# Moving ScalarE's rounding of gated tiles behind the next copy of turned probabilities

## What is computed

```python
for l in range(DEPTH):
    proj = einsum('bld,de->ble', h, w_in[l])
    a, g, zc, q, k, v, za, qi, ki, wi = split(proj)
    u = depthwise_conv(a * sigmoid(g)) + b_dw
    y_conv = silu(layer_norm(u, ln_g, ln_b)) * silu(zc)
    # attention over the 132 keys with the best index score, 8 heads of 64
    y_attn = sparse_attention(q, k, v, top 132 keys) * silu(za)
    y = concatenate([y_conv, y_attn]) @ w_out[l]
    h = layer_norm(alpha * h + y, post_ln_g[l], post_ln_b[l])
```

## Time and profile before

| what | value |
|---|---|
| median of 3 runs | 1014.51 us (1014.0 to 1015.2) |
| profiled execution | 1014.03 us, its span 1012.2 us |
| busy: TensorE | 982.5 us, 97% of the span |
| busy: VectorE | 668.4 us, 66% |
| busy: ScalarE | 559.6 us, 55% |
| busy: GpSimd | 232.4 us, 23% |
| mean granted clock of TensorE | 0.991 |
| attention loop of layer 0 | about 205 to 326 us |
| attention loop of layer 1 | about 514 to 640 us |

### The profile page before, as it was taken

The page is one execution under the profiler, slowest core; times in us unless marked ns, Lnnn a source line. Parts: engine busy times, 40 slices in busy tenths (PEclk is TensorE's granted clock), DMA queues, the critical chain, the costliest instruction groups (busy, mean ns, idle before and its releaser), DMA issues.

```text
span 1012.2 us, 15815 instructions
## 1 busy us (share of the span) xinstructions
PE 982.5 (97%) x6084; PEld 819.3 (81%) x6084; DVE 668.4 (66%) x1444; ACT 559.6 (55%) x920; POOL 232.4 (23%) x254
## 2 busy tenths in 40 slices
PE   8999999999999999999999999999999999999997
PEld 7888998986677988888878677888888788888886
DVE  4899999988673499999988756638522333333432
ACT  6685891655343568598165424544646566564442
POOL 0110671125212401077111511624101000000001
PEclk9999999999999999999999899999999999999999
DMA  8876885752001577487475300478777536366662
GB/s 299 198 183 169 214 195 135 174 118 85 1 1 66 143 186 175 121 192 183 125 170 122 118 21 1 169 172 199 180 215 198 116 87 162 88 162 129 173 160 83
DMA packets 23962, 143.92 MB, mean 142 GB/s; under 512 B 2880, under 2 KB 3648, under 8 KB 8272
## 3 DMA queue, kind: packets, MB, share of 16 engines
q0 software_dynamic: 8496, 60.36, 32.2%
q1 hardware_dynamic: 15392, 82.55, 23.0%
HBM read 140.81 MB, written 2.10 MB: 141 GB/s over the span
## 4 chain that ended last, share of the span: by engine, by line
PE 80%; DVE 10%; ACT 3%; issue 2%; POOL 2%; DMA 2%; SPq 1%; POOLq 0%; DVEq 0%; ACTq 0%
PE psum_B L1404 20%; PE psum_A L1404 13%; PE psum_B L1438 8%; PE psum_A L1438 8%; PE psum_A L1600 6%; DVE conv_acc L1918 4%; PE psum_C L1480 2%; PE psum_C L1404 2%; PE psum_A L1815 2%; PE psum_B L1815 2%; DMA w_raw<-in_weights 2%; PE psum_B L1544 2%; POOL w_lo L1184 2%; PE psum_B L1802 2%; PE psum_A L1516 2%
## 5 line engine op out<-in xcount | busy, mean ns | idle before, releaser
L1191 POOL DMA_DIRECT2D w_lo<-in_weights x59 | 52.0, 881 | 545.9 <-ACT w_lo L728 493.7
L1918 DVE SCALAR_TENSOR_TENSOR conv_acc<-u,vec,conv_acc 128x528 f32<-128x528 f32 (+1 forms) x240 | 172.4, 756 | 3.2
L1404 PE MATMUL psum_B<-x_hi,w_hi 128*128 128x272 f32 (+3 forms) x456 | 138.1, 337 | 0.5 <-ACT shifted L785 0.3
L1404 PE MATMUL psum_B<-x_hi,w_lo 128*128 128x272 f32 (+3 forms) x456 | 135.4, 331 | 0.0
L1404 PE MATMUL psum_B<-x_lo,w_hi 128*128 128x272 f32 (+3 forms) x456 | 135.3, 331 | 0.0
L727 ACT ACTIVATE w_hi<-w_raw 128x2048 fp32r<-128x2048 f32 (+2 forms) x73 | 113.4, 1553 | 25.8 <-DMA w_raw<-in_weights 25.3
L728 ACT ACTIVATE w_lo<-w_raw 128x2048 fp32r<-128x2048 f32 (+2 forms) x73 | 112.7, 1545 | 0.0
L1404 PE MATMUL psum_A<-x_hi,w_hi 128*128 128x272 f32 (+3 forms) x368 | 100.1, 315 | 0.8 <-DMA w_lo<-in_weights 0.4
L1404 PE MATMUL psum_A<-x_lo,w_hi 128*128 128x272 f32 (+3 forms) x368 | 98.1, 309 | 0.0
L1404 PE MATMUL psum_A<-x_hi,w_lo 128*128 128x272 f32 (+3 forms) x368 | 97.9, 309 | 0.0
L1404 PEld LDWEIGHTS psum_B<-x_hi,w_hi 128*128 128x128 f32 (+1 forms) x456 | 79.0, 187 | 10.0 <-issue 1.7
(11 more groups left out here) (409 smaller groups left out, 2294.9 us busy)
## 6 DMA issues: line engine op xcount, KB each, us to landing
w_raw<-in_weights SPq DMA_DIRECT2D x65, 1024.0 KB, 5.0
w_lo<-in_weights POOLq DMA_DIRECT2D x57, 1024.0 KB, 8.3
x_first<-in_x_t SPq DMA_DIRECT2D x8, 264.0 KB, 6.3
h<-in_x SPq DMA_DIRECT2D x1, 2048.0 KB, 9.8
out<-h SPq DMA_DIRECT2D x4, 512.0 KB, 2.6
w_raw<-in_weights SPq DMA_DIRECT2D x2, 512.0 KB, 7.6
post_ln_g<-in_post_ln_g SPq DMA_DIRECT2D x2, 512.0 KB, 4.6
post_ln_b<-in_post_ln_b SPq DMA_DIRECT2D x2, 512.0 KB, 6.3
```

What stands on the lines that cost most here:

```text
L1191: pool.dma_start(wlo[n % RING][:, 0:width], io["weights"][n, :, 0:width], accum_op=ALU.add) \
L1404: mm = pe.matmul(ps[0:cols, i, o:o + b - a], w[wp][:, kt, at:at + cols], x[xp][:, kt, a:b], start=(kt == 0 and wp + xp == 0), stop=(kt == ...
L1918: got = dve.scalar_tensor_tensor(dst, src, w, dst, ALU.mult, ALU.add)
```

## The change

ScalarE's loop used to round gated tiles in `woven`, at the end of a turn and so ahead of the next turn's first copy. Now `woven` leaves the roundings out, and a new function `gated` rounds what the two items of the turn before have, right behind the next turn's first copy and ahead of its two exponentials. The other steps of `woven` (the tanh, the meta rows' pairing, the squares) stay. 16 of the 18 roundings move (9 in layer 0, 7 in layer 1); the last of each layer, behind the loop, stays. The orders of TensorE, VectorE, GpSimd and SP are unchanged.

```diff
--- before.py
+++ after.py
@@ -995,7 +995,10 @@
                             pair_meta((l, part), meta_pair[1], slice(0, CT) if part == "conv" else slice(CT, KD), META)
                         elif op[0] == "tanh":
                             conv_tanh(l, op[1])
-                        elif op[0] == "hi":
+
+                def gated(i):
+                    for op in todo[i]:
+                        if op[0] == "hi":
                             y_hi(l, *op[1:])
 
                 def gates(i):
@@ -1005,6 +1008,9 @@
 
                 for i in range(0, n, 2):
                     take_probs_t(l, i)
+                    if i:
+                        gated(i - 2)
+                        gated(i - 1)
                     if i + 2 < n:
                         exps(l, i + 2)
                         exps(l, i + 3)
```

## The result

The changed kernel takes 1030.8 us (median of 4 runs, 1030.24 to 1032.58) against 1014.66 us before (4 runs, 1014.0 to 1015.2): ratio 1.0171, 95% interval 1.0159 to 1.0184. It is slower, by 16.1 us in the medians. The profiled execution took 1030.28 us; its span grew from 1012.2 to 1028.5 us.

What follows compares the result with a forecast made beforehand. The prediction took TensorE, busy 97% of the span, to bound the kernel. Terms 1.2 + 2.8 + 3.7 + 0.6 + 3.0 + 3.4 = 14.7 us on 1014.03 gave 1028.7, with 0.5 for the median 1029.2; range 1020 to 1035.

Steps and rivals of the forecast that it cites:

- (b): Rival: GpSimd or VectorE has hidden slack, so the copies win; 3.3 us faster, 1011.2 us; chance 0.06.
- (c): Rival: ScalarE's wait at item 14 only changes its line and low parts are absorbed; 1014.5 us; chance 0.06.
- Item 14 of layer 0, 1.2 us: Copy 1.1 us earlier, but turn back 0.8 later, plus 0.4 from item 12's later quarter splits; ends 0.8 and 1.2.
- Items 16 and 17, 2.8: Layer 0: last turn back 1.9 us later through GpSimd's chain, plus 0.9 from L2028 held; ends 1.9 and 2.9.
- Item 18, 3.7: Layer 0: late low weights hold VectorE's gating of the last convolution tile, 3.7 us; low end 1.5, TensorE's wait.
- Item 14 of layer 1, 0.6: GpSimd's deviation comes 0.8 us later, partly covered by 0.36 of slack; 0.6 us, ends 0 and 1.1.
- signs of being wrong: Last turn back under 3 us after item 18's copy, no L1184 or L1211 wait, or item 16's copy no earlier relative to tanh.
- Items 16 and 17 of layer 1, 3.0: TensorE waits for a low part that GpSimd makes behind the low weights; 3.0 us, ends 2.4 and 3.5.
- Clock, 3.4: Two new waits of about 3 us bring two more slow stretches of 1.7 us; ends 0 and 6.8.
- Rival (a): The same chains, but the clock stays up: 11.3 us, 1025.8 us; chance 0.27.
- Eight places at nothing: Items 9, 20, 25, 33 of layer 0 and 9, 12, 18, 25 of layer 1 cost nothing, covered by TensorE's products.
- signs named in the prediction: L863 waits towards 3 us, L2028 waits 6 or more, new L1184 and L1211 waits, L2100 over 1.5, more slow stretches.

Runs made afterwards that it cites:

- the run with the deviation ahead: The whole change, and within an item GpSimd issues the convolution's deviation ahead of the gated tile's low part: 1028.84 us, ratio 1.0148 to the kernel before.
- the run with them ahead: The whole change, and GpSimd issues an item's low weights before its low parts: 1022.24 us, ratio 1.0083 to the kernel before.
- the quiet items alone: The kernel before, roundings moved only at items 9, 20, 25, 33 of layer 0 and 9, 12, 18, 25 of layer 1: 1014.81 us, ratio 1.0009.
- with the product ahead: The kernel before, with TensorE's output product ahead of its turn back in the three items that hold both: 1011.17 us, ratio 0.9974.
- the run with four products: The kernel before, with four more 128x512 SBUF products on GpSimd behind the first residual tile's deviation in layer 0: 1015.01 us, ratio 1.0010.

## Why the prediction was right

The forecast was 1029.2 us, the result 1030.8; rivals (b) and (c) did not come in. The chains through GpSimd's queue are where I had put them; two terms fit partly by luck, and that is said with them. By the steps:

- **Item 14 of layer 0, 1.2 us.** Measured 1.35 less the 0.2 that the span already had at 226: 1.15. The copy was a smaller gain than I wrote (0.46 us instead of 1.1), as the gated tile itself came later: the tanh starts at 235.41, not 234.77. The turn back was late by what the sum had.
- **Items 16 and 17, 2.8.** Measured 4.58 - 1.73 = 2.85. From the copy to the turn back it takes 5.18 us; I had 4.25 and a hold of 0.9. Both halves are there: the rounding's chain and the L2034 of 1.74 us. As the run with the deviation ahead shows, they are not a plain sum: without the chain, 2.5 of 3.2 us of the wait stay.
- **Item 18, 3.7.** Measured 10.81 - 7.04 = 3.77, the high end, by VectorE as I argued, but not by the one hold that I had. The gating was late by 265.68 - 256.25 - 7.04 = 2.4 us before it began, 1.9 of it from a scaling (L2067) held beside the first weight half; its own hold beside the second added 1.5 (2.16 us for 0.69). The sum came out all the same, since both holds end with the weights. TensorE's own wait for the low weights was 1.00, near the low end of 1.5. That the weights' place decides is shown by the run with them ahead.
- **Item 14 of layer 1, 0.6.** This is the term that was mis-sized. From the copy of item 16 to the turn back the delay grew by 12.24 - 10.97 = 1.27 us, over my high end of 1.1. What I had wrong lies ahead of it, in items 9 and 12 of layer 1, which I held at nothing. A scaling held beside item 9's low part (0.77 us instead of 0.45) and the changes around the row at 575.30 make VectorE 0.7 us later (from 10.73 to 11.44 against before), and the trace of the quiet items alone has the same 0.7 there (2.00 to 2.71). Item 14's own step follows, 0.8 (to 12.23), as it is in the trace with that item alone (0.98 to 1.79). So the gated tile came late and the copy of item 16 was no earlier, one of the signs of being wrong that I had named: TensorE's wait for it went from 1.24 to 1.59 us. It didn't show in the end, since by the copy of item 18 the delay is back at 10.74: a slow stretch of 7 us (3.4 us lost) is there before and after, but after it falls partly on the waits. Alone, item 14 costs about 0.6 in its trace and 1.6 [0.6, 2.4] in the medians, where lost clock is 2.0 us more.
- **Items 16 and 17 of layer 1, 3.0.** Measured 3.12, the same low part behind the same low weights.
- **Clock, 3.4.** The sum of lost clock grew by 3.4 us, as much as two stretches of 1.7, and by the table of delays the clock took 0.4 + 2.5 + 1.8 and gave back 1.5: 3.2. At both new waits of 3 us there is a stretch, as I argued, and the two pairs of items alone lost 1.1 + 2.1 = 3.2 us more over their runs. That two such stretches are also the growth between the two traces is partly luck: the one in layer 0 is twice as long as I took it, and one of 1.7 us, at 517, is gone. The executions differ by as much: the kernel before had a mean granted clock of 0.991 to 0.996 over 73 further runs (0.9933 on average), and its trace, at 0.991, is at the low end; the four runs of the changed kernel have 0.987 to 0.988. By these means lost clock grew by about 6 us (13 against 7), the upper end of my term. And the one gap of 1.54 us that I argued from is no rule, as the run with item 18 alone shows. Rival (a), 1025.8, falls by this term.
- **Eight places at nothing.** Within the noise: 0.8 us, interval from -0.2 to 1.9. It does not show that each is nothing: the 0.7 us of items 9 and 12 of layer 1 are VectorE's, and how much of them the kernel pays is open.

The sum of 14.7 us is 1.6 short of the span's 16.3: 0.2 before the first place and 0.6 in the second block, where nothing changed, and the rest item 14 of layer 1. Of the signs named in the prediction, the waits for L863 shrank less than I said (to 3.8, not 3), and the wait for the low weights came as "issue", without their name. All others are in the rows above. Not tried: the change with VectorE's held instructions reading PSUM, so how much of each term is hold and how much queue is known only where the run with the deviation ahead tells them apart.

## What to carry to other kernels

Before an instruction is moved behind another on one engine, list who waits for it and what is queued behind those waiters: here ScalarE's order was improved for one copy, and the price was paid in GpSimd's and VectorE's queues, at places where nothing had been wrong. Here not even the places that did wait gained: moving item 14 alone gave 1.0009 in layer 0 and 1.0015 in layer 1. Look first whether the waiting engine has other work that it could do meanwhile; filling TensorE's wait from its own queue won 2.4 us where moving the rounding lost 16. A gap that a later long product could cover can cost twice when it is left open, once in waiting and once in clock (with the product ahead, lost clock fell by 3.1 us on average).

## What the hardware showed

VectorE's instructions that read and write whole tiles in SBUF alone are held beside GpSimd's elementwise work: 2.16 us for 0.69 (L2106), 2.27 for 0.36 (L2067), 1.74 for 0.75 (L2034), 1.28 to 2.23 in the run with four products; those that read PSUM keep their time (0.69 and 0.67 us). Not everything in SBUF is held. A reciprocal of one column, 0.12 us after the low weights began, kept its 0.15 us:

```profile
262.59 0.15 DVE L2065 RECIPROCAL prob_rsums<-prob_sums 128x1 f32<-128x1 f32 x1
```

GpSimd is held too. The four products took 6.22 us, where four low parts of the same shape would be 4 x 1.27 = 5.1: three of them took 1.27 to 1.30 and one, beside L2143, 2.14. The Trainium skill (SBUF — State Buffer, Who interferes with whom) describes this as one shared port pair, locked for a whole instruction by whichever engine is first, where VectorE takes part with two SBUF inputs or in its fast modes. These rows agree: each held instruction began after GpSimd's and grew by a little less than the rest of it. L2067 at 262.78 had 262.47 + 2.41 - 262.78 = 2.1 us of rest before it and grew by 1.9; L2106 at 265.68 1.6 and 1.5; L2034 at 249.33 1.2 and 1.0; L2143 among the products 1.1 and 0.95. One hold was longer: in the run with the deviation ahead, the scaling at 249.00 began 0.1 us before the first low part ended and grew by 1.1, through the second low part as well.

Beside the low weights there were two holds, one for each half of 2.4 us, with a free instruction that reads PSUM in between.

A slow stretch of TensorE's clock (0.50 of full for 3 to 7 us, the 1.2 GHz level) did not follow a wait of one length. The wait of 1.54 us had one behind it in the kernel before; with item 18 moved alone and with the output product ahead, the same wait had none, though TensorE's order up to it is the same. The traces hold 1.7 to 10.2 us of lost clock; they don't settle what starts a stretch.

Nor does a stretch cost what it loses. In 7 of the 14 traces there is one near the start of layer 1's loop (517 to 520.5 before), in the other 7, the changed kernel among them, there is none. Exactly those without it have this wait, some 13 us behind the place:

```profile
540.38 0.47 PE L1486 MATMUL psum_C<-k,q 64*128 64x272 f32 x1 [1.15 <-DVE neg_max L2058]
```

In the changed kernel VectorE's rows are 10.8 us later than before ahead of the place and 11.1 behind it: nothing was gained by the stretch that is gone, and the wait for masked logits stands in its place. So lost clock summed over windows is no measure of what a kernel would win without it.
